# QKV convolution of the first block: the last tap's product made by ScalarE instead of VectorE

## The chip, the cores and the metric

The kernel runs on one core of a Trainium2 chip. The metric is the device time of one execution in microseconds (us); lower is better. The engines are named as in the profile: PE is TensorE (PEld its weight loads), DVE is VectorE, ACT is ScalarE, POOL is GpSimd and SP is SyncE. Each engine takes its own instructions strictly in the order of the program and waits on semaphores.

## What is computed

The reference runs two layers of a first block (gated delta rule beside a sliding-window attention, then a feed-forward part) and one layer of a second block, on 512 tokens with 1024 channels in float32. What matters here is in the first block, once in each of its two layers:

```python
proj = h @ w_in[l]
dn_qkv, dn_z, dn_a, dn_b, sw_q, sw_k, sw_v, gate_a, gate_b = _split_columns(proj, IN_SIZES)
dn_qkv = jax.nn.silu(causal_dwconv(dn_qkv, dn_conv[l]))     # 3072 channels, 4 taps, causal
...
y_b = swa_sink_attention(sq, sk, sv, swa_sinks[l]) @ w_swa_out[l]
```

For a channel with taps w0 to w3 the convolution gives y[t] = w3 x[t] + w2 x[t-1] + w1 x[t-2] + w0 x[t-3]; the "last tap" is w3, the one without a shift.

## The kernel before

**The stage.** The 3072 channels of `dn_qkv` are 24 tiles of 128 channels by 512 tokens, numbered t = 0 to 23 (`QKV_TILES`); channels lie on partitions, tokens along the row. The same stage runs the sliding-window attention beside the tiles: 16 double units, in steps v = 0 to 18 (three more than 16, since a step scores unit v, turns unit v-2 and multiplies unit v-3 with the values). `slots(t, half)` spreads the 19 steps over the 48 halves of tiles, so a step falls ahead of the convolution of tiles 0, 1, 5, 6, 10, 11, 15, 16, 20 and 21, and behind that of tiles 2, 3, 7, 8, 12, 13, 17, 18 and 22. Steps 0 to 15 hold a `before`, the DVE's work on the scores. Steps 0 to 3 have blocks of 128 keys, the later ones of 256.

**A tile's way through the engines.** Products are made in two parts of float32r, so each weight tile is split. ACT copies the high part (`high`, L218), POOL subtracts it from the whole (`low`, L222), PE runs 24 products into a PSUM bank (`gemm`, L275) and raises `part_made`. DVE then runs `conv(t)` on the bank: the last tap's product into the SBUF tile `big[:, t, :]` (L1154), then the three shifted taps, each read from PSUM and added to that tile (L1157). The third of them raises `evacuated`, which frees the bank: tile t+3 uses the same one. `high` for tile t+2 waits for the product of tile t to be ready, because the buffer of the split weights is shared by every second tile.

**The orders of the queues.** DVE, for each tile: steps of half 0, `conv(t)`, steps of half 1. A DVE step is `keep` (L1136), twice `after` (L1124 to L1130), twice `before` (L1109 to L1119). ACT, for each tile: steps of half 0, `high(t+2)`, steps of half 1; behind the tiles 3, 7, 11, 15 and 19 it runs SiLU on the tiles up to the one before (L1211), which also needs a load of another function table and, for the next Exp, one back. An ACT step is the copies of turned scores (L1183), the store of outputs (L1189), the exponentials of the two units that `before` has just prepared (L1175, L1177), and a split copy of outputs (L1194). Behind the stage PE waits for the last `keep` (semaphore `a_done`), which stands on DVE behind `conv(23)`.

**Lines.** The lines named are L1154 (last tap), L1157 (shifted taps), L1136, L1124, L1116, L1109 and L1119 on DVE, L218, L1175, L1177, L1183, L1194 and L1211 on ACT, L222 on POOL, L275 and L1049 (scores) on PE. The last lines of the kernel hold another ACT copy out of PSUM with a scale for each partition (L2916).

Of the kernel before, what the change touches and what calls it, by code (L numbers as in the profile page):

```python
# [11 lines left out]
ALU = mybir.AluOpType  # L12
ACT = mybir.ActivationFunctionType
# [3 lines left out]
P = 128  # L17
# [92 lines left out]
G_TM, G_SW, G_QKV, G_SO, G_GB, G_GA, G_Z, G_DN, G_WO, G_UP, G_DOWN = 0, 2, 12, 36, 44, 52, 60, 68, 76, 84, 128  # L110
# [22 lines left out]
def build(nc, d, out):  # L133
# [4 lines left out]
    with ExitStack() as ctx:  # L138
        def sb(name, shape, dt=F32):
            return ctx.enter_context(nc.sbuf_tensor(name, shape, dt))  # L140
# [12 lines left out]
        pv = sb("pv", [P, 3 * P])  # L153
# [10 lines left out]
        big = nc.alloc_sbuf_tensor_at("big", [P, 32, T], F32, offset=at_arena)  # L164
# [8 lines left out]
        ps = [ctx.enter_context(nc.psum_tensor(f"ps{b}", [P, T], F32)) for b in range(8)]  # L173
# [132 lines left out]
        with ExitStack() as st:  # L306
            sems, layer_sems = {}, []

            def sem(name):

                if name not in sems:
                    sems[name] = st.enter_context(nc.semaphore(name))
                    layer_sems.append(sems[name].num)
                return sems[name]
# [146 lines left out]
            part_made = sem("part_made")  # L461
            evacuated = [sem(f"evacuated{b}") for b in range(BANKS)]
            tile_in, ada_in = [sem(f"tile_in{e}") for e in range(2)], [sem(f"ada_in{e}") for e in range(2)]
            bank, use = gemm_banks()
# [104 lines left out]
            def slab_of(gt):  # L569

                return SW + (gt - G_SW) // 2 if gt < G_GB else Z + (gt - G_Z) // 2

            def high(act, gt):

                if G_GB <= gt < G_Z:
                    t = gt - G_GB
                    act.wait_ge(tile_in[t % 2], 16 * (t // 2 + 1))
                    act.wait_ge(part_made, gt - 1)
                    nc.scalar.activation(halves(gt, KD)[0], quarter(t % 2, KD), ACT.Copy).then_inc(high_made, 1)  # L579
                else:  # L580
                    make_high(act, slab_of(gt), gt % 2, gt)
# [194 lines left out]
            for l in range(DEPTH):  # L776
# [16 lines left out]
                with nc.Block() as block:  # L793
# [173 lines left out]
                    def _(pool):  # L967
# [14 lines left out]
                    a_scored, a_pre, a_exp, a_post, a_tp, a_tc, a_out, a_kept, a_done = (  # L982
                        sem("a_scored"), sem("a_pre"), sem("a_exp"), sem("a_post"), sem("a_tp"),
                        sem("a_tc"), sem("a_out"), sem("a_kept"), sem("a_done"))
                    c_tap, a_high, zeroed, zeros_out = sem("c_tap"), sem("a_high"), sem("zeroed"), sem("zeros_out")
                    silu_made = sem("silu_made")
                    o_swa = split[:, SPLIT_WK:SPLIT_WK + KD, :], split[:, SPLIT_SQ:SPLIT_SQ + KD, :]
                    zeros = big[:, 30:32, :].rearrange("p a c -> p (a c)")[:, 2 * P:2 * P + ZERO]
# [26 lines left out]
                    def slots(t, half):  # L1015

                        steps = doubles + LAG + 1
                        return [v for v in range(steps) if v * 2 * QKV_TILES // steps == 2 * t + half]
# [81 lines left out]
                    @block.vector  # L1100
                    def _(dve):
                        def before(u):

                            w, par = u % NU // 2, u % 2
                            dve.wait_ge(a_scored, u + 1)
                            if u >= 6:
                                dve.wait_ge(a_tp, u - 5)
                            mask = const("window")[:, 2 * P - width(u):2 * P]
                            nc.vector.scalar_tensor_tensor(  # L1109
                                out=two(s1(u), u), in0=two(ps[4 + u % 2], u), scalar=HD ** -0.5,  # L1110
                                in1=over_heads(mask, 2), op0=ALU.mult, op1=ALU.add).then_inc(a_pre, 1)
                            dve.wait_ge(a_pre, 5 * u + 1)
                            nc.vector.tensor_reduce(st_(u, 0), two(s1(u), u), AX_X, ALU.max).then_inc(a_pre, 1)
                            dve.wait_ge(a_pre, 5 * u + 2)
                            hs = sink[:, 4 * w + par:4 * w + par + 3:2]
                            nc.vector.tensor_tensor(st_(u, 0), st_(u, 0), hs, ALU.max).then_inc(a_pre, 1)  # L1116
                            dve.wait_ge(a_pre, 5 * u + 3)
                            nc.vector.tensor_tensor(st_(u, 1), hs, st_(u, 0), ALU.subtract).then_inc(a_pre, 1)
                            nc.vector.tensor_scalar(st_(u, 2), st_(u, 0), -1.0, None, ALU.mult).then_inc(a_pre, 1)  # L1119

                        def after(u):

                            dve.wait_ge(a_exp, 3 * u + 3)
                            nc.vector.tensor_tensor(st_(u, 4), st_(u, 3), st_(u, 1), ALU.add).then_inc(a_mid, 1)  # L1124
                            dve.wait_ge(a_mid, 2 * u + 1)
                            nc.vector.reciprocal(st_(u, 5), st_(u, 4)).then_inc(a_mid, 1)
                            dve.wait_ge(a_mid, 2 * u + 2)
                            for j in range(2):
                                half = s1(u)[:, width(u) * j:width(u) * (j + 1)]
                                ins = nc.vector.tensor_scalar(half, half, st_(u, 5)[:, j:j + 1], None, ALU.mult)  # L1130
                            ins.then_inc(a_post, 1)

                        def keep(w):
                            m, t, _ = stored(w)
                            dve.wait_ge(a_high, w + 1)
                            nc.vector.tensor_tensor(o_swa[1][:, m, t], sq[:, m, t], o_swa[0][:, m, t], ALU.subtract  # L1136
                                                    ).then_inc(a_done, 1)

                        def step(v):
                            if LAG + 2 <= v:  # L1140
                                keep(v - LAG - 2)
                            if 1 <= v <= doubles:
                                after(2 * v - 2)
                                after(2 * v - 1)
                            if v < doubles:
                                before(2 * v)
                                before(2 * v + 1)

                        def conv(t):
                            gt = G_QKV + t  # L1150
                            y, tile = big[:, t, :], ps[bank[gt]]
                            dve.wait_ge(part_made, gt + 1)
                            w = [pv[:, P + 24 * tap + t:P + 24 * tap + t + 1] for tap in range(4)]
                            nc.vector.tensor_scalar(y, tile[:, :], w[3], None, ALU.mult).then_inc(c_tap, 1)  # L1154
                            for s in (1, 2, 3):
                                dve.wait_ge(c_tap, 3 * t + s)
                                nc.vector.scalar_tensor_tensor(out=y[:, s:], in0=tile[:, 0:T - s], scalar=w[3 - s],  # L1157
                                                               in1=y[:, s:], op0=ALU.mult, op1=ALU.add
                                                               ).then_inc(c_tap if s < 3 else evacuated[bank[gt]], 1)

                        for t in range(QKV_TILES):
                            for v in slots(t, 0):
                                step(v)
                            conv(t)
                            for v in slots(t, 1):
                                step(v)
                        keep(doubles - 1)

                    @block.scalar
                    def _(act):  # L1170
# [25 lines left out]
                        def step(v):  # L1196
# [8 lines left out]
                            if LAG < v <= doubles + LAG:  # L1205
                                store_high(v - LAG - 1)

                        def silu(t):
                            gt = G_QKV + t
                            act.wait_ge(evacuated[bank[gt]], use[gt] + 1)  # L1210
                            nc.scalar.activation(big[:, t, :], big[:, t, :], ACT.Silu).then_inc(silu_made, 1)  # L1211

                        for t in range(QKV_TILES):
                            for v in slots(t, 0):
                                step(v)
                            high(act, G_QKV + t + 2)
                            for v in slots(t, 1):
                                step(v)
                            if t % SILU == SILU - 1 and t + 1 < QKV_TILES:
                                for n in range(max(t - SILU, 0), t):  # L1220
                                    silu(n)
# [1116 lines left out]
        with ExitStack() as st:  # L2338
# [4 lines left out]
            high_made, low_made, part_made = sem("high_made"), sem("low_made"), sem("part_made")  # L2343
            evacuated = [sem(f"evacuated{b}") for b in range(BANKS)]
            bank, use, used = gemm_banks_2()
# [44 lines left out]
            def states(n):  # L2390
# [64 lines left out]
            g_gelu, g_high, g_low, a_times, a_high, a_low, ga_sig, zs_silu, g_mid, g_glu, o_high, o_low, ma_made = (  # L2455
                sem(s) for s in ("g_gelu", "g_high", "g_low", "a_times", "a_high", "a_low", "ga_sig", "zs_silu", "g_mid",
                                 "g_glu", "o_high", "o_low", "ma_made"))
# [739 lines left out]
```

## Time and profile before

| quantity | value |
|---|---|
| device time, median of 3 runs | 2718.33 us (2717.2 to 2724.09) |
| profiled execution, its own time | 2719.56 us |
| span of the profiled execution | 2717.5 us |
| mean granted TensorE clock | 0.977 of full speed |
| PE, DVE, ACT, POOL busy | 2548.1, 1462.7, 1085.1, 918.6 us |
| the stage in layer 0, from conv(0) to conv(23) | 147.42 to 334.94 us |
| the stage in layer 1 | 1276.87 to 1464.42 us |

The span runs from the first to the last instruction of the profiled execution; 2.06 us of its own time lie around it. Busy shares are means over the whole span and say little of one stage: the two stretches of the last rows are what the change touches.

### The profile page before, as it was taken

What the parts mean: (1) busy time and instruction counts of PE and PEld (TensorE: products, weight loads), DVE (VectorE), ACT (ScalarE), POOL (GpSimd) and SP (SyncE); (2) the same over time, 40 slices, a digit from 0 to 9 for tenths busy, and PEclk for the clock granted to TensorE, in tenths of its full rate; (3) what the DMA queues carried; (4) which work ended last, traced back from release to release, by engine and by line L of the source; (5) the groups of instructions that cost most, each with busy time, mean ns of one, the idle gap of its engine ahead of it and who ended that gap; (6) DMA issues with size and microseconds to landing.
All of it is one profiled execution on the core that took longest, in us unless ns stands there. A gap on an engine that the chain in (4) does not pass through costs nothing. (4 is left out here: it accounts for less than half of the span.)

```text
span 2717.5 us, 33405 instructions
## 1 busy us (share of the span) xinstructions
PE 2548.1 (94%) x13185; PEld 2045.5 (75%) x13185; DVE 1462.7 (54%) x2548; ACT 1085.1 (40%) x1904; POOL 918.6 (34%) x400
## 2 busy tenths in 40 slices
PE   5999899999989999989999999998999997999998
PEld 3767777897867888766777777877888886776787
DVE  6299848654545545545996562264444207736323
ACT  3445554235332232133555533543333223336432
POOL 1532322112434444335223221243444443322343
PEclk8999999999999999999999999999999998999999
DMA  7211326634324426532213152322222324831232
GB/s 255 63 63 63 125 70 172 186 125 143 104 98 140 140 93 211 179 117 62 78 57 130 47 139 64 136 93 78 93 94 93 108 91 124 160 106 44 70 124 78
DMA packets 331390, 300.00 MB, mean 110 GB/s; under 512 B 56718, under 2 KB 302820, under 8 KB 330212
## 3 DMA queue, kind: packets, MB, share of 16 engines
q1 hardware_dynamic: 279268, 279.52, 32.5%
q10 hardware_dynamic: 51968, 18.35, 2.6%
q8 instruction: 105, 1.72, 0.3%
q14 instruction: 49, 0.40, 0.0%
HBM read 267.92 MB, written 29.93 MB: 110 GB/s over the span
## 5 line engine op out<-in xcount | busy, mean ns | idle before, releaser
L275 PE MATMUL ps<-hh,split 128*128 128x512 f32 x3808 | 1283.3, 404 | 42.0 <-POOL split L222 30.5
L222 POOL TENSOR_TENSOR split<-ring,split 128x1024 fp32r<-128x1024 f32 (+2 forms) x340 | 810.7, 2386 | 1365.4 <-ACT split L218 1326.9
L275 PEld LDWEIGHTS ps<-hh,split 128*128 128x128 f32 x3808 | 721.8, 190 | 214.2 <-POOL split L222 47.5
L275 PE MATMUL ps<-hl,split 128*128 128x512 f32 x1904 | 748.0, 393 | 0.0
L218 ACT ACTIVATE split<-ring 128x1024 fp32r<-128x1024 f32 (+1 forms) x336 | 341.2, 1017 | 869.9 <-PE ps L275 668.5
L275 PEld LDWEIGHTS ps<-hl,split 128*128 128x128 f32 x1904 | 362.1, 190 | 72.2 <-issue 8.4
L275 PE MATMUL ps<-split 128*128 128x512 f32 x1152 | 284.4, 404 | 9.6 <-DVE split L1136 7.7
L275 PEld LDWEIGHTS ps<-split 128*128 128x128 f32 x1152 | 218.2, 190 | 70.8 <-issue 14.4
L2276 PE MATMUL ps<-split 128*128 128x512 f32 x1056 | 248.2, 398 | 0.0
L2276 PEld LDWEIGHTS ps<-split 128*128 128x128 f32 x1056 | 202.8, 193 | 42.7
L587 POOL TENSOR_TENSOR split<-ring,split 128x1024 fp32r<-128x1024 f32 x32 | 76.5, 2390 | 313.6 <-ACT split L579 313.6
L2134 DVE TENSOR_TENSOR wk<-wk,ps 128x512 f32<-128x512 f32 x44 | 30.3, 688 | 180.6 <-PE ps L275 180.6
L1157 DVE SCALAR_TENSOR_TENSOR big<-ps,pv,big 128x511 f32<-128x511 f32 x144 | 107.8, 748 | 5.1
L2312 DVE SCALAR_TENSOR_TENSOR x<-ps,mod,x 128x512 f32<-128x512 f32 x16 | 12.0, 749 | 131.5 <-PE ps L2276 131.5
L1175 ACT ACTIVATE big<-big 128x256 f32<-128x256 f32 (+1 forms) x88 | 41.5, 472 | 94.0 <-DVE big L1119 94.0
L363 DVE SCALAR_TENSOR_TENSOR kd<-spare,c_act,kd 128x512 f32<-128x512 f32 x56 | 61.8, 1104 | 28.9 <-DMA spare<-in_w_ada_dram 27.1
L2123 DVE TENSOR_SCALAR wk<-ps,pv 128x512 f32<-128x512 f32 x44 | 33.0, 749 | 77.0 <-PE ps L275 70.3
L2138 DVE TENSOR_TENSOR split<-wk,split 128x512 fp32r<-128x512 f32 x44 | 71.2, 1619 | 5.6 <-ACT split L2170 5.6
L1291 DVE TENSOR_TENSOR big<-big,wk 128x512 f32<-128x512 f32 x32 | 39.2, 1225 | 64.8 <-ACT wk L1273 64.8
L2126 DVE SCALAR_TENSOR_TENSOR wk<-ps,pv,wk 128x511 f32<-128x511 f32 x88 | 65.9, 749 | 3.1
L491 DVE SCALAR_TENSOR_TENSOR vs<-ring,c_act,vs 128x256 f32<-128x256 f32 x112 | 63.8, 570 | 1.3 <-DMA ring<-in_w_ada_dram 0.2
L956 DVE SCALAR_TENSOR_TENSOR wk<-ps,pv,wk 128x512 f32<-128x512 f32 x20 | 15.0, 751 | 90.0 <-ACT wk L890 90.0
(427 smaller groups left out, 3258.8 us busy)
## 6 DMA issues: line engine op xcount, KB each, us to landing
ring<-in_w_in_dram SPq DMA_DIRECT2D x60, 1024.0 KB, 5.0
ring<-in_w_up_dram SPq DMA_DIRECT2D x44, 1024.0 KB, 5.0
ring<-in_w_in_dram SPq DMA_DIRECT2D x34, 512.0 KB, 5.0
big<-in_w_ada_dram SPq DMA_DIRECT2D x16, 1024.0 KB, 8.4
ring<-in_w_ada_dram SPq DMA_DIRECT2D x32, 512.0 KB, 3.6
spare<-in_w_ada_dram SPq DMA_DIRECT2D x16, 1024.0 KB, 7.5
ring<-in_w_down_dram SPq DMA_DIRECT2D x16, 896.0 KB, 5.3
ring<-in_w_swa_out_dram SPq DMA_DIRECT2D x8, 1024.0 KB, 5.2
```

Source lines behind the costliest of these rows:

```text
L218: nc.scalar.activation(halves(pt, nk)[0], slot(n, nk)[:, :, e * P:(e + 1) * P], ACT.Copy).then_inc(high_made, 1)
L222: on.tensor_tensor(halves(pt, nk)[1], slot(n, nk)[:, :, e * P:(e + 1) * P], halves(pt, nk)[0], ALU.subtract).then_inc(low_made, 1)
L275: ins = nc.tensor.matmul(ps[bank[gt]][0:m, :], w[:, k, :], r[:, k, :], start=(k == 0 and w is w_high and r is rhs[0]), stop=(k == nk - 1 a ...
L363: nc.vector.scalar_tensor_tensor(out=acc, in0=w, scalar=c_act[:, k:k + 1], in1=acc, op0=ALU.mult, op1=ALU.add).then_inc(first_added, 1)
L491: nc.vector.scalar_tensor_tensor(out=acc, in0=w, scalar=c_act[:, k:k + 1], in1=acc, op0=ALU.mult, op1=ALU.add).then_inc(ada_added, 1)
L587: nc.gpsimd.tensor_tensor(halves(gt, KD)[1], quarter((gt - G_GB) % 2, KD), halves(gt, KD)[0], ALU.subtract).then_inc(low_made, 1)
L1157: nc.vector.scalar_tensor_tensor(out=y[:, s:], in0=tile[:, 0:T - s], scalar=w[3 - s], in1=y[:, s:], op0=ALU.mult, op1=ALU.add).then_inc(c_ ...
L1175: nc.scalar.activation(half, half, ACT.Exp, bias=st_(u, 2)[:, j:j + 1], accum_out=st_(u, 3)[:, j:j + 1]).then_inc(a_exp, 1)
L1291: nc.vector.tensor_tensor(tile, tile, wk[:, 10 + n % 2, :], ALU.mult).then_inc(n_scaled, 1)
L2126: nc.vector.scalar_tensor_tensor(out=y[:, s:], in0=ps_[:, 0:T - s], scalar=w[2 - s], in1=y[:, s:], op0=ALU.mult, op1=ALU.add).then_inc(u_t ...
L2138: nc.vector.tensor_tensor(g_low[:, ds(j + 4 * i, 1), :], wk[:, 8 + j % 4, :].unsqueeze(1), g_high[:, ds(j + 4 * i, 1), :], ALU.subtract).t ...
L2276: ins = nc.tensor.matmul(ps[bank[gt]][:, :], w[:, k, :], r[:, k0 + k, :], start=(k0 + k == 0 and w is w_high and r is g_high), stop=(k0 + ...
```

## The change

ACT makes the last tap's product with a copy out of PSUM that has a scale for each partition, and raises a new semaphore `c_first`. It does so in its own queue right behind `high(t+2)`. DVE's first instruction of `conv(t)` goes, and its first shifted tap waits for `c_first`. The count on `c_tap` is adjusted from three to two for each tile.

```diff
-                    c_tap, a_high, zeroed, zeros_out = sem("c_tap"), sem("a_high"), sem("zeroed"), sem("zeros_out")
+                    c_first, c_tap, a_high, zeroed, zeros_out = (sem("c_first"), sem("c_tap"), sem("a_high"), sem("zeroed"),
+                                                                 sem("zeros_out"))
@@ conv(t), VectorE
                             dve.wait_ge(part_made, gt + 1)
-                            w = [pv[:, P + 24 * tap + t:P + 24 * tap + t + 1] for tap in range(4)]
-                            nc.vector.tensor_scalar(y, tile[:, :], w[3], None, ALU.mult).then_inc(c_tap, 1)
+                            w = [pv[:, P + 24 * tap + t:P + 24 * tap + t + 1] for tap in range(3)]
+                            dve.wait_ge(c_first, t + 1)
                             for s in (1, 2, 3):
-                                dve.wait_ge(c_tap, 3 * t + s)
+                                if s > 1:
+                                    dve.wait_ge(c_tap, 2 * t + s - 1)
                                 nc.vector.scalar_tensor_tensor(out=y[:, s:], in0=tile[:, 0:T - s], scalar=w[3 - s],
@@ ScalarE
+                        def last_tap(t):
+                            gt = G_QKV + t
+                            act.wait_ge(part_made, gt + 1)
+                            nc.scalar.activation(big[:, t, :], ps[bank[gt]][:, :], ACT.Copy,
+                                                 scale=pv[:, P + 72 + t:P + 73 + t]).then_inc(c_first, 1)
+
@@ the loop over tiles, ScalarE
                                 step(v)
                             high(act, G_QKV + t + 2)
+                            last_tap(t)
                             for v in slots(t, 1):
                                 step(v)
```

## Rows read from the trace of the kernel before

**Rows 1.** Busy time in both stretches: us, then PE, PEld, DVE, ACT, POOL, clock, DMA.

```profile
147.42:334.94 187.52, 174.07 (x998) 134.55 (x996) 173.06 (x387) 103.68 (x270) 54.90 (x23) 0.99 0.26 85
1276.87:1464.42 187.55, 174.12 (x998) 134.51 (x997) 173.08 (x387) 103.69 (x271) 54.97 (x23) 0.99 0.26 85
```

**Rows 2.** Waits of PE, 146 to 322 us: us in total, times, longest.

```profile
PE ps L275 <- POOL split L222: 9.1, 8, 1.7
PE ps L1049 <- DVE big L1109: 3.2, 2, 2.1
PE ps L1049 <- DVE wk L1109: 1.1, 1, 1.1
```

**Rows 3.** Timeline of tile 18: start us, us, engine, line, operation, [idle before].

```profile
299.15 0.74 DVE L1154 TENSOR_SCALAR big<-ps,pv 128x512 f32<-128x512 f32 x1
...
299.93 2.32 DVE L1157 SCALAR_TENSOR_TENSOR big<-ps,pv,big 128x511 f32<-128x511 f32 x3
...
300.68 1.04 ACT L218 ACTIVATE split<-ring 128x1024 fp32r<-128x1024 f32 x1
301.62 1.06 ACT L1183 ACTIVATE wk<-ps 128x512 f32<-128x512 f32 x2
301.80 2.40 POOL L222 TENSOR_TENSOR split<-ring,split 128x1024 fp32r<-128x1024 f32 x1 [8.25 <-ACT split L218]
302.16 2.33 DVE L1136 TENSOR_TENSOR split<-sq,split 128x256 fp32r<-128x256 f32 x1
...
304.41 0.15 DVE L1124 TENSOR_TENSOR big<-big 128x2 f32<-128x2 f32 x1
```

**Rows 4.** One line, L1157, all 144: shortest, median, longest ns, first and last start.

```profile
L1157 DVE SCALAR_TENSOR_TENSOR big<-ps,pv,big x144: 746/748/751, 148.2 to 1466.8; 128x511 f32<-128x511 f32 x48, 128x510 f32<-128x510 f32 x48, 128x509 f32<-128x509 f32 x48
```

**Rows 5.** DVE groups by shape, 147.4 to 322 us: busy, mean ns, idle before.

```profile
L1136 DVE TENSOR_TENSOR split<-sq,split 128x256 fp32r<-128x256 f32 x14 | 24.3, 1738 | 0.0
...
L1124 DVE TENSOR_TENSOR big<-big 128x2 f32<-128x2 f32 x32 | 10.5, 328 | 0.0
...
L1116 DVE TENSOR_TENSOR big<-big,sink 128x2 f32<-128x2 f32 x30 | 7.9, 263 | 1.0
```

**Rows 6.** One line, L1136, both layers: shortest, median, longest ns.

```profile
L1136 DVE TENSOR_TENSOR split<-sq,split x32: 414/1958/2341, 178.1 to 1467.4; 128x256 fp32r<-128x256 f32 x32
```

**Rows 7.** One line, L2916, copies out of PSUM with a scale per partition.

```profile
L2916 ACT ACTIVATE b_rows_out<-ps,vs x4: 679/688/694, 2709.6 to 2711.3; 128x512 f32<-128x512 f32 x4
```

**Rows 8.** Timeline: the same four instructions, merged.

```profile
2709.55 2.42 ACT L2916 ACTIVATE b_rows_out<-ps,vs 128x512 f32<-128x512 f32 x4
```

**Rows 9.** Timeline: conv and split copy at tiles 0, 4, 8, 11 and 12.

```profile
147.42 0.75 DVE L1154 TENSOR_SCALAR big<-ps,pv 128x512 f32<-128x512 f32 x1
...
148.43 1.04 ACT L218 ACTIVATE split<-ring 128x1024 fp32r<-128x1024 f32 x1
...
175.12 0.74 DVE L1154 TENSOR_SCALAR big<-ps,pv 128x512 f32<-128x512 f32 x1
...
179.42 1.04 ACT L218 ACTIVATE split<-ring 128x1024 fp32r<-128x1024 f32 x1
...
208.49 0.74 DVE L1154 TENSOR_SCALAR big<-ps,pv 128x512 f32<-128x512 f32 x1
...
213.53 1.05 ACT L218 ACTIVATE split<-ring 128x1024 fp32r<-128x1024 f32 x1
...
240.30 0.74 DVE L1154 TENSOR_SCALAR big<-ps,pv 128x512 f32<-128x512 f32 x1
...
246.28 1.04 ACT L218 ACTIVATE split<-ring 128x1024 fp32r<-128x1024 f32 x1
```

**Rows 10.** Timeline of the stage's end in layer 0.

```profile
334.94 1.06 ACT L218 ACTIVATE split<-ring 128x1024 fp32r<-128x1024 f32 x1 [4.82 <-PE ps L275]
...
337.96 0.75 DVE L1136 TENSOR_TENSOR split<-sq,split 128x256 fp32r<-128x256 f32 x1
...
338.77 4.45 PE L275 MATMUL ps<-split 128*128 128x512 f32 x12 [3.87 <-DVE split L1136]
```

## Prediction

> **What bounds the kernel now.** I read the stage's busy time first. In both layers it lasts 187.5 us from the first conv to the last, with PE busy 174.1 and DVE 173.1 [rows 1]; the layers agree within 0.1 us in every column, so I work one out and double it. Two engines at the same 92% don't say which sets the pace, so the waits come next. PE waits 9.1 us for POOL's low parts and 3.2 + 1.1 us for DVE to free the score banks, 13.4 us in all [rows 2]. POOL in turn had stood 8.25 us for ACT's split copy [rows 3], and ACT, busy 103.7 of 187.5 us, copies it only when DVE has prepared its exponentials. DVE's groups have next to no idle time ahead of them (0.0, 0.0, 1.0 us over 175 us [rows 5]): its queue is the chain, and ACT, POOL and PE follow it. The timeline then shows how one tile runs [rows 3]. DVE ends the step at B = 299.15 and goes straight on to the conv: 0.78 us for the last tap, 2.23 us for the three shifted ones, so it reaches `keep` at B + 3.01. ACT still works on the second pair of exponentials and a store, starts `high` at B + 1.53, and is free for the next instruction 0.94 us later. POOL's `low` runs from B + 2.65 for 2.40 us.
>
> One thing more is in these rows. `keep` (L1136) took 2.33 us there, while its shortest is 0.414 [rows 3, 6], and ended as POOL's `low` did. DVE waits for POOL inside the instruction, so this time counts as busy. L1124 and L1116, which take 0.15 us when free [rows 3], have the same in their means. Per layer up to 322 us these waits are 14 x (1.738 - 0.414) = 18.5 us, 32 x (0.328 - 0.15) = 5.7 and 30 x (0.263 - 0.16) = 3.1, together 27.3 us [rows 5, 6]. The shifted taps, which read PSUM and only one tile of SBUF, show none of it: all 144 lie between 746 and 751 ns, whatever POOL does [rows 4].
>
> **The change part by part.** *Removed from DVE:* 0.78 us for each of 24 tiles, 18.7 us a layer. Were ACT's product always there in time, PE's own 13.4 us of waits would cap the gain.
>
> *Added to ACT:* one copy out of PSUM with a scale for each partition. The nearest row is the very same kind: 688 ns from start to end [rows 7], and (2.42 - 0.69)/3 = 0.58 us of the queue [rows 8]. ACT is busy 103.7 of 187.5 us [rows 1], so 24 x 0.58 = 14 us more don't make it the bound.
>
> The Trainium skill ("ScalarE: Activation LUTs", What ACT_TABLE_LOAD costs) says that each operand given per partition adds about 93 ns to an activation; by that and its 186 ns + 0.833 ns per element the copy would be an estimated 0.71 us, and the sum below 0.6 us larger over both layers.
>
> *Moved:* the product changes from a queue that is ready for it to one that isn't. It stands behind `high(t+2)`, so with h as the time from B to the start of `high`, DVE's first shifted tap can start at B + h + 0.94 + 0.69 + 0.08. The 0.08 is the step from one engine to another that `high` and `low` show (ends 301.72, starts 301.80 [rows 3]). The conv ends at B + h + 1.71 + 2.23, against B + 3.01: it is late by h + 0.93. Behind DVE's new wait stand `keep`, `after` and the next `before`, hence ACT's next exponentials, the next `high`, POOL and PE: everything. Where two convs follow each other with no step between, the second product is made under the first's taps, and the pair is late by h + 1.71 + 4.46 - 6.02 = h + 0.15.
>
> The tiles, up to tile 18:
> - 7 with a wide `before` ahead (5, 9, 10, 13, 14, 15, 18), h = 1.53: 7 x 2.46 = 17.2 us.
> - 2 with a narrow one (0, 3), h = 148.43 - 147.42 = 1.01 [rows 9]: 2 x 1.94 = 3.9.
> - Tiles 4 and 8, where the table load and the SiLUs stand ahead of `high`: h = 4.30 and 5.04 [rows 9], late by 5.2 and 6.0.
> - Pairs 1/2, 6/7 and 16/17: 1.16 + 2 x 1.68 = 4.5.
> - Pair 11/12, with SiLUs between: `high(14)` starts at B + 5.98 [rows 9], now 0.58 later, and the second product waits for it. 6.56 + 1.71 + 2.23 - 6.02 = 4.5.
>
> Together 41.3 us of lateness at the ends of the convs. But the wait for POOL that stood behind them goes: `low` keeps its place after `high` and ends at h + 1.12 + 2.40 = h + 3.52, the taps now at h + 3.94 (pairs, with two `low` behind each other: h + 5.92 against h + 6.17). POOL's stretch lies inside the taps, which it doesn't hold up, and `keep` or L1124 meets it no more. Of the 27.3 us I take off the last two `keep` (behind tiles 19 and 20, which no longer set the end), 2 x 1.32: 24.6 us come back. Net 41.3 - 24.6 = 16.7 us a layer.
>
> The Trainium skill ("SBUF — State Buffer", Who interferes with whom) states this as a rule: a DVE instruction with two SBUF inputs contends with a GpSimd instruction that reads SBUF, one with at most one SBUF input doesn't. The rows agree (0.414 to 2.341 us against 746 to 751 ns); by the rule the 24.6 us come back as in the sum, without it they would not.
>
> *The end.* The last three convs wait for PE. From there PE sets the time, late by the 16.7 us with which `high(21)` came. At the end, `high(25)` and the product stand ahead of the taps: 334.94 + 1.71 + 2.23 = 338.88, `keep` 0.42 more, 339.30 against 338.71 [rows 10]; PE waits for just that: + 0.6.
>
> *At nothing:* 0.58 us more of ACT ahead of its copies and stores, covered by its idle 84 us a layer (without that cover it would be up to 14 us); one semaphore; banks freed later, but conv(t) ends long before PE needs the bank for tile t+3 (at tile 8, nearly two steps of some 10 us). The SP queue isn't touched.
>
> Sum: 2 x (16.7 + 0.6) = 34.6 us. On the profiled execution's own 2719.6 that is 2754.2, on the median 2718.3, 1.3 us below it, 2752.9.
>
> *Bounds.* The copy may take from its 0.58 us of queue to some 0.75, the step from 0 to 0.2: with 14 places a layer, 28 in all, from -5 to +5 us. PE's longer pauses may lower its clock for stretches; it has the slack by then, and I allow + 5. If POOL's stretch slips past the taps in the narrow margin of 0.4 us at one tile in three, up to + 5. Own range 2745 to 2768.
>
> **The rivals.**
> - *The lateness counts in full.* If the waits for POOL only moved on to other two-input instructions, nothing would come back: 2 x (41.3 + 0.9) = 84.4, 2803 us. For it: POOL's work is the same and DVE's two-input instructions too. Against it: in the one layout the stretch lies under the taps. Chance 0.05; something between the two, 2770 to 2800, 0.05.
> - *Faster: PE becomes the bound.* If ACT's product were ready when DVE arrives, DVE would save 0.78 us a tile and PE would lose its 13.4 us a layer: 2718.3 - 26.8 = 2691.5. It decides by the lag h + 1.71: below 0.78 us the change gains. The smallest I read is 2.7 us, so only second tiles of pairs gain. Chance 0.06. The Trainium skill ("VectorE: DVE Perf Modes", Rules for kernel authors) would point this way: for chained VectorE instructions it says to have fewer of them and not to mind the semaphores; here the row with h speaks against.
> - *No change.* A tile costs nothing where h + 0.93 is no more than the wait for POOL that it takes away, 2.33 - 0.41 = 1.92 us at a wide tile. The wide tiles miss that by 0.54 us only, the SiLU tiles by 3 to 4. Were all of it covered, or taken up by the stage behind, the time would be 2718. Against it: PE waits 3.87 us for the last `keep` with nothing else to do [rows 10], so what is late there stays late. Chance 0.05.
>
> **How the numbers follow.** Forecast 0.79, in between 0.05, in full 0.05, none 0.05, faster 0.06. The predicted time is the forecast's, 2753 us. The forecast's own range holds some 0.72 of its 0.79; widened to 2737 to 2770, below for a queue of ACT that runs ahead at the tiles with SiLU (15.7 us of the 41.3), above for the first of the cases in between, it holds a little over 0.8. A measurement here tells no less than 0.3% (8 us) from no change. Faster 0.06, same 0.05, slower 0.89.
>
> **What would show it.** The stage should last some 204 us instead of 187.5, each layer the same. DVE busy should fall by 18.7 + 24.6 us a layer, and DVE should show waits for ACT at L1157 with some 3.2 us at wide tiles, 6 to 7 at tiles 4 and 8. L1136 should be near 0.42 us throughout. The new copy on ACT should take 0.69 us. PE's waits should grow by about 17 us a layer. The prediction is wrong if L1136 still shows 2.3 us, if DVE's waits for ACT are below 1 us, or if POOL's `low` starts later after `high` than now.

## The result, and the profile after

| kernel | median us | ratio to before, 95% interval | stage, layers 0 and 1 |
|---|---|---|---|
| before | 2717.8 | | 193.8, 193.8 us |
| changed | 2757.3 (2756.27 to 2758.45) | 1.0139 [1.0126, 1.0151] | 212.0, 211.7 us |

The change costs 39.5 us; forecast were 34.6, and 2753 for the measured 2757. (The median of the kernel before has one more run in it here than the 2718.33 from which the forecast started.) The last column is a measure that I use for all runs: from DVE's first score instruction of the stage to the end of the last `keep`, in the profiled execution; it starts some 2.5 us ahead of `conv(0)` and ends 4 to 5 us behind the stretches of [rows 1], so it is longer than they are. It grew by 18.2 + 17.8 = 36.0 us, of the 38.9 by which the span grew (2717.5 to 2756.4). The rest lies outside the stage: 0.3 us ahead of it, -1.4 between the two stages (935.65 to 934.24) and +3.9 behind the second (1249.3 to 1253.2).

The same stretches as in [rows 1], busy time in layer 0 and 1 from the point where DVE is free for `conv(0)` to the end of PE's part for `conv(23)`, at which the last split copy starts:

```profile
147.75:352.50 204.75, 180.38 (x998) 138.47 (x996) 129.98 (x364) 116.32 (x293) 54.86 (x23) 0.96 0.24 78
1294.00:1498.78 204.78, 180.71 (x998) 138.66 (x996) 129.97 (x364) 116.30 (x293) 54.82 (x23) 0.96 0.24 78
```

The stretch is 204.8 us long instead of 187.5, while DVE's busy time fell from 173.1 to 130.0: an engine became 43 us less busy and the stage 17 us longer, so that its idle time grew by 60 us. The granted clock went from 0.99 to 0.96. Two groups of waits show where that time goes. DVE's own, 146 to 350 us, and PE's, 147.75 to 352.5 us, against [rows 2]:

```profile
DVE big L1159 <- ACT big L1213: 65.6, 20, 6.7
```

```profile
PE ps L275 <- POOL split L222: 13.6, 8, 2.5
PE ps L1050 <- DVE big L1110: 8.3, 3, 4.4
PE ps L1050 <- DVE wk L1110: 2.3, 3, 2.0
```

DVE, which had next to no idle time, now stands 65.6 us before its first shifted tap (L1159 is the old L1157), 20 times, at most 6.7 us. PE waits for 24.2 us instead of 13.4. That is 10.8 us more, and not the 17 that the prediction gave as a sign: the other 6.3 us of the longer stretch are in PE's busy time, 180.4 instead of 174.1 for the same 998 matmul instructions, at the lower granted clock. The timeline of tile 18, the one of [rows 3], names the steps:

```profile
316.08 0.16 DVE L1120 TENSOR_SCALAR big<-big 128x2 f32<-128x2 f32 x1
316.28 0.51 ACT L1177 ACTIVATE wk<-wk,big 128x256 f32<-128x256 f32 x1 [0.59 <-DVE big L1120]
...
317.37 0.40 ACT L1196 ACTIVATE split<-sq 128x256 fp32r<-128x256 f32 x1
317.68 1.04 ACT L218 ACTIVATE split<-ring 128x1024 fp32r<-128x1024 f32 x1
318.62 0.67 ACT L1213 ACTIVATE big<-ps,pv 128x512 f32<-128x512 f32 x1
318.80 2.42 POOL L222 TENSOR_TENSOR split<-ring,split 128x1024 fp32r<-128x1024 f32 x1 [8.77 <-ACT split L218]
...
319.41 2.32 DVE L1159 SCALAR_TENSOR_TENSOR big<-ps,pv,big 128x511 f32<-128x511 f32 x3 [3.16 <-ACT big L1213]
...
321.64 0.42 DVE L1137 TENSOR_TENSOR split<-sq,split 128x256 fp32r<-128x256 f32 x1
321.97 0.16 DVE L1125 TENSOR_TENSOR big<-big 128x2 f32<-128x2 f32 x1
```

In [rows 3] the conv began 0.07 us after L1119's start; the same here gives B = 316.15. `high` starts at B + 1.53 and the product at B + 2.47, both to the hundredth as worked out ahead; the product takes 0.67 us (0.69 expected), the step to DVE 0.12 (0.08), and the taps start at B + 3.26 (3.24). POOL's stretch, 318.80 to 321.22, begins while DVE waits and ends inside the taps (319.41 to 321.73), and `keep` takes its 0.42 us. It does so everywhere. One line each, all 32 `keep` and all 144 shifted taps, against [rows 6] and [rows 4]:

```profile
L1137 DVE TENSOR_TENSOR split<-sq,split x32: 414/417/418, 185.4 to 1502.8; 128x256 fp32r<-128x256 f32 x32
```

```profile
L1159 DVE SCALAR_TENSOR_TENSOR big<-ps,pv,big x144: 742/749/753, 150.5 to 1502.1; 128x511 f32<-128x511 f32 x48, 128x510 f32<-128x510 f32 x48, 128x509 f32<-128x509 f32 x48
```

The longest `keep` fell from 2341 to 418 ns; the taps, under which POOL's stretch now ends, are at 742 to 753. Of the prediction's three signs of being wrong none came: `keep` is short, DVE's waits for ACT are 2.1 us and more, and POOL's `low` starts 1.12 us after `high`, as before (318.80 - 317.68, and 301.80 - 300.68 in [rows 3]). The two waits that I had put at 6 to 7 us, tiles 4 and 8 in DVE's timeline:

```profile
183.13 2.31 DVE L1159 SCALAR_TENSOR_TENSOR big<-ps,pv,big 128x511 f32<-128x511 f32 x3 [5.94 <-ACT big L1213]
...
222.30 2.32 DVE L1159 SCALAR_TENSOR_TENSOR big<-ps,pv,big 128x511 f32<-128x511 f32 x3 [6.67 <-ACT big L1213]
```

### The profile page after: what moved, and what is told of

It is laid out like the page before. It is cut to its first block and busy times, and to the rows that moved or that the text cites. A ratio compares the mean times of both kernels' runs of the same rounds, so it can differ in the third digit from the quotient of the medians.

```text
span 2756.4 us, 33453 instructions
## 1 busy us (share of the span) xinstructions
PE 2563.0 (93%) x13185; PEld 2055.1 (75%) x13185; DVE 1377.4 (50%) x2500; ACT 1112.7 (40%) x1952; POOL 918.9 (33%) x400
## 5 line engine op out<-in xcount | busy, mean ns | idle before, releaser
L2285 PEld LDWEIGHTS ps<-split 128*128 128x128 f32 x1056 | 198.9, 189 | 41.3
L1159 DVE SCALAR_TENSOR_TENSOR big<-ps,pv,big 128x511 f32<-128x511 f32 x144 | 107.3, 749 | 142.9 <-ACT big L1213 139.5
```

The costliest lines, as they stand in the source:

```text
L2285: ins = nc.tensor.matmul(ps[bank[gt]][:, :], w[:, k, :], r[:, k0 + k, :], start=(k0 + k == 0 and w is w_high and r is g_high), stop=(k0 + ...
```

## The experiments

All ratios are to the kernel before, with which each ran on the same chip. "Stage" is as above, layer 0 and layer 1; before has 193.8 in both, the changed kernel 212.0 and 211.7. The ratios are those on record and differ from the quotients of the medians by up to 0.0012.

**SiLU moved.** From the changed kernel:

```diff
-                            if t % SILU == SILU - 1 and t + 1 < QKV_TILES:
-                                for n in range(max(t - SILU, 0), t):
+                            if t % 5 == 4:
+                                for n in range(max(t - 5, 0), t):
                                     silu(n)
-                        for t in range(QKV_TILES - SILU - 1, QKV_TILES):
+                        for t in range(19, QKV_TILES):
                             silu(t)
```

> The changed kernel with the four SiLU batches behind tiles 4, 9, 14 and 19 instead of 3, 7, 11, 15 and 19, so that none stands ahead of a product for which VectorE already waits. Theory (the cost is the lag of ACT's queue ahead of the product): tiles 4 and 8 fall from 5.9 and 6.7 us of wait to 3.2 or less and the second wait of pair 11/12 (2.7 us) goes; about 3.4 + 3.7 + 1.8 = 8.9 us a layer, 17.7 in all, so 2757.3 - 17.7 = 2740 us, range 2735 to 2745. Rival (the time is set by PE or by the waits for POOL, and the lag at these tiles is hidden): no change, 2755 to 2759.

Measured 2739.9 us, ratio 1.0088 [1.0071, 1.0104]; stage 203.1 and 202.7. The wait at tile 4 is down to 2.95 us, and of those after it only the ones at tiles 22 and 23, where PE sets the time, exceed 3.2 us (3.5 and 4.1). It is the forecast to the microsecond, 8.9 us a layer: the lag at three places (tiles 4, 8 and the pair 11/12) made up nearly half of the loss.

**Product ahead of the split copy.** From the changed kernel:

```diff
-                            high(act, G_QKV + t + 2)
                             last_tap(t)
+                            high(act, G_QKV + t + 2)
```

> The changed kernel with ACT's product one place earlier, ahead of the split copy. It is ready 0.94 us sooner at every tile. Theory (lag and the wait for POOL together): the taps start 0.94 us sooner, but the split copy and with it POOL's stretch come 0.58 us later, the taps end before POOL does and keep (L1137) waits for POOL again, some 1.3 us instead of 0.42 in all; each wide tile ends up 0.13 us later, pairs 0.3, the end 0.6: 2757 + 5 = 2762, range 2755 to 2766. Rival (lag alone, POOL's stretch plays no part): 14 places a layer less 0.94 us, 2757 - 26 = 2731.

Measured 2763.9 us, 1.0174 [1.0158, 1.0191]; stage 212.3 in both layers. Its timeline at tile 18:

```profile
318.41 0.67 ACT L1213 ACTIVATE big<-ps,pv 128x512 f32<-128x512 f32 x1
318.98 1.05 ACT L218 ACTIVATE split<-ring 128x1024 fp32r<-128x1024 f32 x1
319.19 2.31 DVE L1159 SCALAR_TENSOR_TENSOR big<-ps,pv,big 128x511 f32<-128x511 f32 x3 [2.21 <-ACT big L1213]
...
320.11 2.40 POOL L222 TENSOR_TENSOR split<-ring,split 128x1024 fp32r<-128x1024 f32 x1 [8.84 <-ACT split L218]
...
321.43 1.37 DVE L1137 TENSOR_TENSOR split<-sq,split 128x256 fp32r<-128x256 f32 x1
```

DVE's wait is shorter by 0.95 us, 2.21 instead of 3.16, and `keep` longer by just that, 1.37 instead of 0.42: it ends when POOL does. DVE's waits for ACT fell by 16.6 us in the layer (65.6 to 49.0) and the stage didn't get shorter by any of it; over both layers `keep` lies between 0.97 and 1.46 us. The 2762 us expected were met in part by luck: of the 5 us the stages account for 0.9, the rest of the profile's 7.8 us lies outside them. This is the run that shows the second half of the mechanism: at these tiles the end is set by whichever comes later, the taps or POOL's stretch.

**Product twice.** From the changed kernel, with the counts on `c_first` doubled:

```diff
+                            for n in (1, 2):
+                                nc.scalar.activation(big[:, t, :], ps[bank[gt]][:, :], ACT.Copy,
+                                                     scale=pv[:, P + 72 + t:P + 73 + t]).then_inc(c_first, 1)
+                                if n == 1:
+                                    act.wait_ge(c_first, 2 * t + 1)
```

> The changed kernel with ACT's product made twice, the second after the first; VectorE waits for the second. Lag longer by about 0.75 us at 14 to 15 places a layer (0.67 and a step). Theory: no wait for POOL is left to take it up, so it counts in full: 2757 + 21 = 2778, range 2774 to 2784. Rival (much of the lag is still hidden behind POOL or PE): under 2767.

Measured 2780.0 us, 1.0235 [1.0215, 1.0254]; stage 224.9 and 224.6, 12.9 a layer more than the changed kernel. At a wide single tile DVE waits 3.89 us instead of 3.16; 0.73 us at 14 or 15 places are 10 to 11 us a layer, and PE's busy time in the stage of layer 0 is 2.1 us longer (185.0 against 182.9). On this side nothing is left to take a lag up.

**Wait only.** From the kernel before:

```diff
                             dve.wait_ge(part_made, gt + 1)
+                            dve.wait_ge(high_made, gt + 3)
                             w = [pv[:, P + 24 * tap + t:P + 24 * tap + t + 1] for tap in range(4)]
```

> The kernel before, VectorE making the last tap's product itself, with one wait added: conv(t) starts only when ACT has ended the split copy of tile t+2. ACT does no product. Theory (the cost is where DVE has to stand in ACT's queue, not the copy as work): each single conv is late by h + 1.14 us against h + 0.97 in the changed kernel, pairs by 0.95 more than there, the wait for POOL vanishes as well: 2757 + 9 = 2766, range 2759 to 2771. Rival (the cost is the copy as ACT's work, or its reading of PSUM beside VectorE): near the kernel before, 2717 to 2725.

Measured 2765.2 us, 1.0165 [1.0138, 1.0191]; stage 216.7 and 216.7. `keep` is at 414 to 418 ns here too. No work was moved and none added, and the loss is larger than with the change, by 4.7 and 5.0 us a layer where about 4.5 were expected. The copy as ACT's work isn't what costs.

**Split copy and product ahead of the exponentials.** From the changed kernel, `rest(v)` being the second half of `step(v)` (exponentials and the split copy of outputs):

```diff
+                        owed = []
                         for t in range(QKV_TILES):
                             for v in slots(t, 0):
                                 step(v)
+                                owed.append(v)
                             high(act, G_QKV + t + 2)
                             last_tap(t)
-                            for v in slots(t, 1):
+                            for v in owed:
+                                rest(v)
+                            owed = list(slots(t, 1))
+                            for v in owed:
                                 step(v)
```

> The changed kernel with ACT's order turned round: for each tile the split copy and the product stand ahead of the exponentials of the step that VectorE runs before that tile's conv, instead of behind them. Then the product of tile t is ready before VectorE asks for it at all tiles but 12. Theory: VectorE saves its 0.78 us a tile, PE's waits of 13.4 us a layer become the cap: below the kernel before, 2690 to 2710, most likely 2698. Rival (the product must wait for PE anyway, or POOL's stretch falls on VectorE's other instructions and takes the gain): 2715 to 2730; if ACT's exponentials become late, above 2740.

Measured 2707.3 us, 0.9967 [0.9955, 0.9978]; stage 186.0 and 189.3. Below the kernel before, at the upper end of the range: in layer 0 the product is still late at tile 12 (5.15 us), at tiles 14 and 17 (2.5 and 3.1) and at nine others by 0.5 to 1.2 us.

**The same order, DVE making its product.** The edit to `step` and the loop of the last run, on the kernel before.

> The kernel before, no product on ACT, with ACT's order turned round as in the early run: the split copy stands ahead of the exponentials. It asks how much of that run's 10 us is the order alone. Theory (PE is the bound there, since DVE stood idle for 25 us in layer 0's stage, more than the 15 to 18 us of products it gets back): the same time or a little less, since the last conv needn't wait for ACT (0.95 us a layer): 2706, range 2700 to 2712. Rival (the product taken off DVE brings the gain, the order only makes it possible): near the kernel before, 2714 to 2718.

Measured 2718.4 us, 0.9998 [0.9982, 1.0013]; stage 191.4 and 189.5. My theory was wrong, the rival right for the time as a whole. The stages by themselves are shorter than before, by 2.4 and 4.4 us; in the profile the rest of the execution is 5.5 us longer, which I can't explain. PE's waits in layer 0, 146 to 322 us:

```profile
PE ps L1049 <- DVE big L1109: 8.9, 4, 4.5
PE ps L1049 <- DVE kd L948: 3.3, 1, 3.3
PE ps L1049 <- DVE wk L1109: 2.2, 2, 1.4
```

They no longer go to POOL but to DVE; the wait on L948 (at 147.0 us) lies ahead of the stage, so that 11.1 us are inside it. I had counted DVE's idle time of the early run as free for the product. Much of it isn't: of its 32.5 us of waits for ACT's product in layer 0, 15.4 stand ahead of tiles 20 to 23, at the stage's end, and it has none at tiles 3 to 6, where PE waits 1.8 us for DVE to free a score bank.

**Early order and moved SiLU, three forms.** With the product behind the split copy (the early run with the SiLU edit):

> The early run with the SiLU batches behind tiles 4, 9, 14 and 19. The wait of 5.2 us at tile 12 goes, but PE is the bound: between nothing and 4 us a layer, 2704, range 2699 to 2708.

Measured 2708.5 us, 0.9957 [0.9940, 0.9973]; stage 188.5 and 187.4: no further gain, and just outside the range. With the product ahead of the split copy:

> As the run with the early order and moved SiLU, and the product ahead of the split copy. The last conv's product is ready 0.95 us sooner, the split copies come 0.58 us later, which PE doesn't need: one to two us a layer less, 2702, range 2697 to 2707.

Measured 2692.9 us, 0.9893 [0.9873, 0.9914]; stage 179.5 and 179.7, far more than expected. Busy time and PE's waits in layer 0:

```profile
147.70:320.90 173.20, 171.02 (x1000) 134.09 (x998) 141.95 (x366) 111.18 (x294) 52.63 (x22) 1.00 0.29 92
```

```profile
PE ps L1050 <- DVE big L1110: 1.1, 2, 0.8
PE ps L1050 <- DVE wk L1110: 0.9, 2, 0.6
```

PE is busy 171.0 of 173.2 us, its waits are 2.0 instead of 13.4, the clock is 1.00. DVE waits for the product at only two of the tiles up to 19 (0.8 and 0.4 us). That is the case that the prediction gave as its rival "faster", 2691.5 by the cap of PE's waits. That the two numbers lie so close is in part luck: 13.4 us a layer isn't a cap, the stages became 14.3 and 14.2 us shorter, since PE's busy time in them fell too (176.6 to 173.2 in layer 0). And without ACT's product, DVE doing it:

> The kernel before, VectorE making its product itself, with both orders of the fastest run so far: split copies ahead of the exponentials and SiLU behind tiles 4, 9, 14 and 19. Against the run of 2693 us it lacks only the product on ACT. Theory (the product taken off DVE is needed, as the early order alone brought nothing): DVE's queue stays the bound, only tile 12's stall goes: 2713, range 2708 to 2718. Rival (the moved SiLU brings it): 2690 to 2700.

Measured 2724.0 us, 1.0032 [1.0019, 1.0044]; stage 197.6 and 190.4. That is above the range of the theory (2708 to 2718) and far from the rival's. Both orders together bring nothing without the product on ACT; they cost a little. In layer 0 of this run DVE waits 9.1 us for PE at the convs and PE 14.4 us for DVE inside the stage, each in its turn.

**Product first in the early order, SiLU where it was.**

> The changed kernel with the product and then the split copy ahead of the exponentials, SiLU batches where they were. It parts the two differences between the early run (2707) and the fastest one (2693). If the product's place ahead of the split copy matters, because it stands on DVE's path and the split copy doesn't: 2694 to 2699, with only tile 12's stall of some 4 us a layer partly back. If both were needed: 2703 to 2707.

Measured 2701.6 us, 0.9947 [0.9929, 0.9965]; stage 184.3 in both layers. The time lies between the two cases expected. The place ahead of the split copy is worth 1.7 and 5.0 us in the two layers by itself (against 186.0 and 189.3), the moved SiLU 4.7 more on top; in the form with the product behind, the moved SiLU was worth nothing.

## Why the prediction was right

**The bound.** DVE's queue was the chain of the stage: the wait-only run, which adds nothing but a wait to that queue, lengthens the stage by 22.9 us in each layer.

**The price of the copy.** 0.69 us expected, 0.67 measured; ACT's busy time rose by 12.6 us a layer and, by the wait-only run, which came out as expected without it, cost nothing that shows.

**The lag.** h + 1.71 was worked out, h + 1.73 measured at tile 18. At the other kinds of tile the sum gives 2.7, 6.0 and 6.8 us (narrow, 4, 8); the waits, which begin about 0.1 us later, came at 2.65, 5.94 and 6.67. The run with SiLU moved confirms the terms of tiles 4, 8 and 11/12 as a group: 8.9 us a layer expected from the waits of the changed kernel, 8.9 and 9.0 measured.

**What came back from POOL.** 24.6 us a layer were taken off the lateness of 41.3. DVE's busy time fell by 43.1 us, 18.7 + 24.6 = 43.3 expected; with the waits for POOL left in place it would have been about 18. The run with the product first shows the exchange: DVE's busy time in the stage of layer 0 is 152.6 us there against 134.9 in the changed kernel, its waits for ACT 16.6 less, and the stage equally long.

**The size.** 34.6 us were forecast and 39.5 measured. Of the difference of 4.9, some 1.4 are in the stages: 36.0 against 34.6, or 17.2 to the last `high` (16.7 expected) and 1.0 and 0.6 behind it (0.6). The step from ACT to DVE, sized at 0.08 us from ACT to POOL, measured 0.12, the copy 0.02 less than its 0.69; together 0.02 x 14 = 0.3 a layer. The rest I had not counted: the profiled execution is 2.8 us longer outside the stages, and the median a little more than the profile. In the profiles of the other runs the stretch behind the second stage is 1250.9 to 1256.3 us long, in that of before 1249.3, so this part varies from run to run with no difference in its code. It varies with PE's busy time: the same 6366 matmul instructions behind the second stage took 1186.5 us before and 1191.9 in the changed kernel. Whether a part of it belongs to the change I can't tell.

**What was wrong in it.** Not a term of the sum but a sign: PE's waits were to grow by about 17 us a layer and grew by 10.8. The stretch did grow by the 17 us; the prediction had them all as waits and allowed for the clock only in its bounds, while 6.3 us of them are PE's busy time.

**The rivals.** "Lateness in full" (2803) fell with `keep` at 418 ns. "No change" fell with the stage. "Faster" named its condition, a lag below 0.78 us, and the run with the early order, the product first and the moved SiLU meets it at nearly all tiles: there the same product on ACT takes the kernel to 2692.9 us.

**What stays open.** Against the early run, the product ahead of the split copy shortens both stages together by 6.8 us, the moved SiLU by nothing (-0.5), and the two at once by 16.2. The traces show where it goes but not why: from the run with moved SiLU alone to the fastest, the stage of layer 0 falls by 8.9 us, of which 4.1 are PE's waits inside it (6.1 to 2.0; one of 4.5 us for a score bank is gone) and 4.4 its busy time, 177.6 to 173.2 for the same 1008 matmul instructions at a granted clock of 0.97 and 0.99. With both orders and DVE's product, layer 0 takes 7.2 us more than layer 1; 6.1 of them are PE's waits (14.4 against 8.3), whose cause I didn't follow.

## What to carry to other kernels

Work moved to another engine has to stand in that engine's queue, and whoever needs it stands there with it. Read where in the other queue the new instruction stands at the moment when the first engine wants it, and how long the instructions ahead of it take; the busy shares say nothing of this. Here 37 us of work (18.7 a layer) off the chain that set the pace cost 39.5 us behind the exponentials, and the same 37 us off it brought 26 us once ACT's queue was turned round. The order alone brought nothing to the time (2718.4 and 2724.0), nor did the product alone.

An instruction that is slow because it waits inside itself for another engine, as `keep` did here, hides slack: the first part of a new wait in front of it is free, up to the length of that hidden wait (1.9 us here), and taking just that part of the new wait away gives nothing back either.

## What the runs showed of the hardware

The hold by POOL isn't limited to DVE instructions with two inputs in SBUF. Some with one input lengthen as well, when they start together with POOL's stretch. From the run with both orders and DVE's product, layer 0, by timeline and then by groups of one shape, 146 to 340 us:

```profile
193.46 2.40 POOL L222 TENSOR_TENSOR split<-ring,split 128x1024 fp32r<-128x1024 f32 x1 [4.83 <-ACT split L218]
193.48 2.80 DVE L1130 TENSOR_SCALAR big<-big 128x256 f32<-128x256 f32 x2
...
264.26 2.37 POOL L222 TENSOR_TENSOR split<-ring,split 128x1024 fp32r<-128x1024 f32 x1 [6.88 <-ACT split L218]
264.29 2.37 DVE L1119 TENSOR_SCALAR big<-big 128x2 f32<-128x2 f32 x1
```

```profile
L1130 DVE TENSOR_SCALAR big<-big 128x256 f32<-128x256 f32 x32 | 14.3, 488 | 0.6
...
L1119 DVE TENSOR_SCALAR big<-big 128x2 f32<-128x2 f32 x32 | 7.4, 230 | 0.0
```

L1130 and L1119 multiply one SBUF tile by a scalar. L1119 takes 2.37 us there instead of its usual 0.16, and ends as POOL does; the pair of L1130 takes 2.80 instead of 0.62. In the early order without the moved SiLU, where none is caught, the means are 351 and 161 ns; here they are 488 and 230, and it is two instructions of the 32 and one of the 32 that raise them. That fits the Trainium skill ("SBUF — State Buffer", Who interferes with whom), which counts scalar instructions of one SBUF input among those that can take the shared ports. The prediction gave that section's rule without this exception; its sum doesn't use it, since the shifted taps read PSUM, and those reads never showed a hold (737 to 753 ns for both kinds of tap in the changed kernel, the fastest run and this one).

In the stage of the changed kernel, with PE's waits up from 13.4 to 24.2 us, the granted clock was 0.96, in the fastest run, with 2.0 us of waits, 1.00. The two go together in these traces; no run separates them.
